# A decoder on one core: the FFN's first weight tile rounded in the GLA stage, router weights as left operand, the first scatter of zeros left out, and some reorderings in the attention stage

## The reference, cut to what matters

```python
def rms_norm(x, g):
    xf = x.astype(jnp.float32)
    y = xf * lax.rsqrt(jnp.mean(xf * xf, axis=-1, keepdims=True) + RMS_EPS)
    return (y * g.astype(jnp.float32)).astype(x.dtype)

def swiglu(h, w_gate, w_up, w_down):
    return (jax.nn.silu(h @ w_gate) * (h @ w_up)) @ w_down

def moe_swiglu(h, w_router, w_gate, w_up, w_down):
    logits = (h @ w_router).astype(jnp.float32)
    top_val, top_idx = lax.top_k(logits, TOP_K)            # 2 of 8
    top_w = jax.nn.softmax(top_val, axis=-1)
    gates = jnp.sum(jax.nn.one_hot(top_idx, N_EXPERTS, dtype=jnp.float32) * top_w[..., None], axis=-2)
    out = jnp.zeros_like(h)
    for e in range(N_EXPERTS):
        y = swiglu(h, w_gate[e], w_up[e], w_down[e])
        out = out + gates[..., e:e + 1].astype(h.dtype) * y
    return out
# first block, per layer: h = h + mixer(rms_norm(h)); h = h + ffn_or_moe(rms_norm(h))
```

## Time and profile before

| | |
|---|---|
| median of 3 runs (lowest, highest) | 2160.39 us (2160.05, 2161.13) |
| the profiled execution: its time, its span | 2161.18 us, 2159.4 us |
| PE, DVE, ACT busy, share of the span | 98%, 76%, 65% |
| mean granted TensorE clock | 0.992 |

### The profile page before, as it was taken

The page is one execution under the profiler, slowest core; times in us unless marked ns, Lnnn a source line. Parts: engine busy times, 40 slices in busy tenths (PEclk is TensorE's granted clock), DMA queues, the critical chain, the costliest instruction groups (busy, mean ns, idle before and its releaser), DMA issues.

```text
span 2159.4 us, 26580 instructions
## 1 busy us (share of the span) xinstructions
PE 2114.2 (98%) x10002; PEld 1732.1 (80%) x10003; DVE 1647.9 (76%) x2373; ACT 1397.8 (65%) x2006; POOL 25.5 (1%) x28
## 2 busy tenths in 40 slices
PE   8999999989999999999999999989999999999998
PEld 6778888778888888888888888878778788787886
DVE  5655556779999999999999999985656776565675
ACT  6554447467777777777777777765446665455664
POOL 0000000000000000000000000000110000020000
PEclk9999999989999999999999999999999999999999
DMA  6345543269999899999999899954434445443433
GB/s 270 136 168 189 195 176 137 78 269 374 372 358 386 328 376 355 367 343 371 374 354 370 339 376 360 371 206 156 167 136 140 144 170 181 176 148 136 147 139 115
DMA packets 77510, 537.24 MB, mean 249 GB/s; under 512 B 10672, under 2 KB 10928, under 8 KB 12736
## 3 DMA queue, kind: packets, MB, share of 16 engines
q1 hardware_dynamic: 77088, 535.38, 66.1%
q10 hardware_dynamic: 288, 0.10, 0.0%
HBM read 534.40 MB, written 1.05 MB: 248 GB/s over the span
## 4 chain that ended last, share of the span: by engine, by line
PE 95%; DVE 3%; ACT 1%; issue 1%; DMA 0%; ACTq 0%; DVEq 0%
PE bank L235 28%; PE bank L237 28%; PE bank L236 28%; PE bank L755 4%; PE bank L2488 1%; PE bank L2487 1%; PE bank L1845 1%; PE bank L1869 1%; DVE w_low L210 1%; DVE w_low L213 0%; PE bank L2533 0%; PE bank L2532 0%; DVE xT_low L480 0%; ACT xT_high L470 0%; PE bank L2531 0%
## 5 line engine op out<-in xcount | busy, mean ns | idle before, releaser
L235 PE MATMUL bank<-w_high,xT_high 128*128 128x512 f32 x1072 | 429.9, 401 | 12.1 <-DVE w_low L210 5.8
L210 DVE TENSOR_TENSOR w_low<-ring,w_high 128x1024 fp32r<-128x1024 f32 x232 | 285.3, 1230 | 188.3 <-ACT w_high L202 183.2
L237 PE MATMUL bank<-w_high,xT_low 128*128 128x512 f32 x1072 | 421.1, 393 | 0.0
L236 PE MATMUL bank<-w_low,xT_high 128*128 128x512 f32 x1072 | 420.5, 392 | 0.0
L202 ACT ACTIVATE w_high<-ring 128x1024 fp32r<-128x1024 f32 x232 | 245.4, 1058 | 219.7 <-PE bank L237 210.1
L235 PE MATMUL bank<-w_high,moe_x_high 128*128 128x512 f32 x896 | 359.0, 401 | 1.8 <-DVE moe_x_low L1861 1.8
L237 PE MATMUL bank<-w_high,moe_x_low 128*128 128x512 f32 x896 | 350.4, 391 | 0.0
L236 PE MATMUL bank<-w_low,moe_x_high 128*128 128x512 f32 x896 | 349.7, 390 | 0.0
L213 DVE TENSOR_TENSOR w_low<-ring,w_high 128x1024 fp32r<-128x1024 f32 x232 | 284.8, 1228 | 0.0
L235 PEld LDWEIGHTS bank<-w_high,xT_high 128*128 128x128 f32 x1072 | 203.3, 190 | 57.5 <-issue 10.4
L205 ACT ACTIVATE w_high<-ring 128x1024 fp32r<-128x1024 f32 x232 | 243.0, 1047 | 0.0
(11 more groups left out here) (345 smaller groups left out, 3119.5 us busy)
## 6 DMA issues: line engine op xcount, KB each, us to landing
moe_ring<-in_moe_tiles SPq DMA_DIRECT2D x144, 1024.0 KB, 5.6
ring<-in_hy_tiles SPq DMA_DIRECT2D x103, 1024.0 KB, 4.7
ring<-in_moe_tiles SPq DMA_DIRECT2D x96, 1024.0 KB, 5.5
ring_wide<-in_moe_tiles SPq DMA_DIRECT2D x96, 1024.0 KB, 5.6
ring<-in_ffn_tiles SPq DMA_DIRECT2D x17, 1024.0 KB, 4.8
ring_wide<-in_ffn_tiles SPq DMA_DIRECT2D x16, 1024.0 KB, 4.8
ring_wide<-in_gla_in_tiles SPq DMA_DIRECT2D x6, 1024.0 KB, 8.9
ring<-in_sb_in_tiles SPq DMA_DIRECT2D x6, 1024.0 KB, 4.8
```

The lines of the kernel that those rows point to most:

```text
L210: self.nc.vector.tensor_tensor(self.low[:, place, FIRST], memory[:, FIRST], self.high[:, place, FIRST].bitcast(F32), ALU.subtract).then_in ...
L235: nc.tensor.matmul(out, x[0], w[0], start=start, stop=False, **more)
L236: nc.tensor.matmul(out, x[0], w[1], start=False, stop=False, **more)
L237: return nc.tensor.matmul(out, x[1], w[0], start=False, stop=stop, **more)
```

## The change

What it does, by place:

- **GLA's end**: ACT and DVE do tile 16 (the FFN's first) ahead of turning h's first half.
- **FFN's start**: TensorE transposes h's second half after half of `gate_up(0, 0)` (row group 0). ACT and DVE do only tile 17 ahead of the squares and of h's second half; root and reciprocal follow, and only then tile 18.
- **Attention**: DVE's `block_out(3)` comes ahead of tile 9's split, `take_k(2)` and `scaled(2)` ahead of tile 10's, `take_q(2)` ahead of tile 10's rounding. The last values go ahead of the third part of the output product on TensorE, and `o_high`, `o_low` ahead of the last tile on ACT and DVE.
- **Route**: the router's 8 columns become the stationary operand, 256 columns of xT are streamed: 24 matmuls, which give the logits transposed (8 x 256). DVE copies them out, TensorE transposes them back (2 small ones). DVE does comparisons before it makes the rows; ACT does its exponential before it rounds the rows; the rows' low parts come after the selection matrix.
- **Experts**: the first gather goes by row groups: all 16 matmuls of the first half of every bank by t=0, then t=1, and then the same for the second half. The zeroing on DVE, the scatter of zeros and its additions are gone.

```diff
@@ GLA: act
-                tiles(16)
+                tiles(17)
                 tail.act(act, 0)
@@ ffn: pe, gate_up
+                        if (c, half, t) == (0, 0, 0):
+                            head.pe(pe, 1)
...
                     gate_up(c, 0)
-                    if c == 0:
-                        head.pe(pe, 1)
-                    else:
+                    if c:
                         turn(c - 1)
@@ ffn: act (dve alike, with total, dve, dve_rest)
-                W.prepare(act, "act", first + SPLIT)
+                W.prepare(act, "act", first + 2)
                 head.squares(act, 1)
                 head.act(act, 1)
+                head.act_rest(act)
+                head.scaled(act)
+                W.prepare(act, "act", first + SPLIT)
...
-                    if c == 0:
-                        head.act_rest(act)
-                        head.scaled(act)
@@ stick_breaking: pe
-                tile_out(1, 0, 0)
                 values(2)
                 values(3)
+                tile_out(1, 0, 0)
@@ stick_breaking: act
+                take_q(2)
                 tiles(11)
-                take_q(2)
...
-                tiles(16)
                 o_high(2)
                 o_high(3)
+                tiles(16)
@@ stick_breaking: dve
                 stayed(0)
+                block_out(3)
                 tiles(10)
                 stayed(1)
-                block_out(3)
+                take_k(2)
                 weighed(0)
                 weighed(1)
+                scaled(2)
                 tiles(11)
-                take_k(2)
-                scaled(2)
...
-                tiles(16)
                 o_low(2)
                 o_low(3)
+                tiles(16)
@@ moe: gather, first pair only
+            if by_rows:
+                for odd in range(2):
+                    for t in range(TT):
+                        pe.wait_ge(K.s_xn, t + 1)
+                        for g, b in enumerate(GATHERED):
+                            for i in range(2):
+                                last = nc.tensor.matmul(B[b][:, odd * 2 * P:(odd + 1) * 2 * P], rows[i][:, t, (2 * g + odd) * P:(2 * g + odd + 1) * P],
+                                                        sel[:, t, :], start=((i, t) == (0, 0)), stop=((i, t) == (1, 1)))
+                            if odd and t:
+                                last.then_inc(G.gath, 1)
+                return
@@ moe: dve
-                for x in y:
-                    nc.vector.memset(x[:].bitcast(F32), 0.0).then_inc(G.yv, 1)
-                nc.vector.memset(selT[:].bitcast(F32), 0.0).then_inc(G.gst, 1)
@@ moe: pe (dve alike; the counts in the waits follow)
-                    pe_run(pe, G, pair, pair, lambda: scatter(pe, G, pair * 2), ...)
-                scatter(pe, G, E)
+                    pe_run(pe, G, pair, pair, lambda: scatter(pe, G, pair * 2 - 1) if pair else None, ...)
+                scatter(pe, G, E - 1)
@@ route: pe
+                for k in range(KC):
+                    if k % 4 == 0:
+                        for t in range(TT):
+                            head.operand(pe, k // 4, t)
+                    last = matmul3(nc, B[0][0:E, 0:S], tuple(w[:, k, :] for w in K.wr), tuple(x[:, k, :] for x in K.xT),
+                                   start=(k == 0), stop=(k == KC - 1))
+                last.then_inc(s_mm, 1)
+                pe.wait_ge(s_lgT, 1)
                 for t in range(TT):
-                    for k in range(KC):
...
+                    last = nc.tensor.transpose(B[1][:, 4 * E + t * E:4 * E + (t + 1) * E], lgT[:, t * P:(t + 1) * P], K.ident[0:E, 0:E])
@@ route: dve
+                dve.wait_ge(s_mm, 1)
+                nc.vector.tensor_copy(lgT[:], B[0][0:E, 0:S]).then_inc(s_lgT, 1)
                 head.scaled(dve)
...   (logits, comparisons and choice as before; then:)
+                for t in range(TT):
+                    nc.vector.scalar_tensor_tensor(out=K.xn[:, t, :], ...).then_inc(s_rows, 1)
...   (slot numbers, selection matrix; then:)
+                for t in range(TT):
+                    dve.wait_ge(s_high, t + 1)
+                    nc.vector.tensor_tensor(rows[1][:, t, :], ..., ALU.subtract).then_inc(s_xn, 1)
```

More of the change, by code:

```diff
@@ L1349, in add @@
                     nc.vector.tensor_tensor(hv, B[2 * t + n][:], hv, ALU.add).then_inc(f["added"], 1)
-                W.prepare(dve, "dve", first + SPLIT)
+                W.prepare(dve, "dve", first + 2)
                 head.total(dve)
                 head.dve(dve, 1)
+                head.dve_rest(dve)
+                head.scaled(dve)
+                W.prepare(dve, "dve", first + SPLIT)
                 for c in range(N):
@@ L1763, with __init__ @@
 class ExpertSems:
-    def __init__(self, nc, ctx, prefix, stream, first, value, start):
+    def __init__(self, nc, ctx, prefix, stream, first, value, scattered_before):
         (self.sel, self.gath, self.xh, self.xg, self.silu, self.hid, self.tp, self.hh, self.hT, self.ya, self.yv, self.gps,
@@ L1931, in turn_sel @@
             def turn_sel(q):
-                if G.start:
-                    pe.wait_ge(G.add, n * 8 + 4 * q + 4)
-                elif q:
-                    pe.wait_ge(G.add, n * 8 + 4)
+                if G.scattered_before(n, q):
+                    pe.wait_ge(G.add, n * 8 + 4 * q)
                 mine = sel[:, :, q * P:(q + 1) * P].bitcast(F32)
@@ L1950, in pe_run @@
                     pe.wait_ge(G.hT, n * STEPS + N + 1)
-                    scatter(pe, G, n * 2 + G.start)
+                    scatter(pe, G, n * 2)
                 if s == STEPS - 1:
```

57 lines of the change are left out of this document (24 added, 33 removed).

## The result

| | before | after |
|---|---|---|
| median (lowest, highest), 4 runs each | 2160.22 us (2160.05, 2161.13) | 2146.90 us (2146.68, 2147.99) |
| the profiled execution: time, span | 2161.18, 2159.4 | 2147.04, 2145.2 |
| mean granted TensorE clock | 0.992 | 0.995 |

First, the page of after, part 1, beside the earlier trace rows: PE's share is as before, with 30 matmuls fewer.

A forecast was written before the change was run, and what follows sets the result against it. TensorE, busy 98% of the span, was taken as the bound. Gains of 4.2 (FFN), 3.9 (attention), 2.0 (route) and 2.1 (zeros), less 0.1, took 2160.4 to 2148.3 us; range 2145.8 to 2152.0.

The forecast's parts named there:

- FFN's start: At the FFN's start: two PE waits and a slow stretch go, a 1.9 us wait on hid comes; gain 4.2 us.
- Table switches: Rival at the FFN's start: ACT's two table switches hold it longer, hid 2.6 us later, 2150.9 us; chance 0.04.
- Attention: In the attention's middle and end: reordering removes PE's waits; gain 3.9 us, from 2.6 to 4.1.
- score(3)'s 0.4 of margin: In the attention: take_k(3) ends at 392.5, score(3) wants it at 392.9; missed, it costs up to 1 us.
- Route: From router to first expert matmul: earlier logits and gather bring that matmul from 463.98 to 462.0; gain 2.0 us.
- slow for 3.8 us, then 0.12 each: In the first gather: the old matmul rhythm is assumed to stay, putting the 26th matmul at 459.9.
- Zeros: At the experts' start: 8 matmuls fewer give 1.8 us, and a shorter wait for hid makes it 2.1 us.
- without them it isn't the limit: In the route: the memsets (2.1 us) were in DVE's way; once gone, DVE does not limit the first expert matmul.
- The slow clock: Rival in gather and FFN: gather stays slow, 1.8 us; FFN's new wait adds 1.5; 2149.8 to 2151.6 us; chance 0.20.
- the better case: Rival: clock up early in the gather, x at 461.6, FFN's hid half a us sooner; 2147.0 us; chance 0.10.
- Experts at DMA's pace: Rival in the experts' stage: DMA sets the pace, first refill 2.4 us earlier, not 4.1; 2150.0 us; chance 0.05.
- splits that lag: Rival in the experts' stage: DVE's split work exceeds PE's step and the lag stays; 2168 us at 102%; chance 0.01.

The follow-up runs named there:

- f_tile: The changed kernel with tile 16 rounded and split in the FFN's program again, the new order there kept; 2151.23 us.
- silu_first: The changed kernel with the first silu and hidden ahead of tile 19's rounding and split in the FFN; 2146.98 us.
- the five siblings: u_att2, u_att1, f_tile, silu_first and u_ffn: the changed kernel's route, instruction for instruction, with edits elsewhere; slower gathers; medians 2146.98 to 2152.71 us.
- u_route: The changed kernel with the whole route part undone (48 narrow matmuls, old order, gather by banks), zeros still left out; 2148.13 us.
- b_nozero: The kernel before with only the zeroing, the scatter of zeros and its additions removed; 2157.78 us, ratio 0.9986.
- u_ffn: The changed kernel with its FFN part undone: tile 16 rounded in the FFN's program again, old order there; 2152.71 us.
- u_att1: The changed kernel with the attention's middle undone (block_out(3), take_k(2), scaled(2), take_q(2) in their old places); 2151.07 us.
- u_att2: The changed kernel with the attention's end undone (output product's third part ahead of the last values, last tile's split ahead of the last output split); 2149.54 us.
- u_zero: The changed kernel with the memsets, the scatter of zeros and its additions put back; 2153.90 us.
- r_prod: The changed kernel with only the router's product undone (48 matmuls, xT stationary, 8 columns streamed), new order and gather kept; 2150.56 us.

## Why the prediction was right, and where not

- **FFN's start: right, 4.35 for 4.2.** The chain was forecast stone by stone, and each came within 0.2 us of its place once the 0.8 of the start is added back: transposes 134.32 (134.3), copies 134.96 (135.0), tiles from 138.88 (139.0), load 142.8 (142.9), hid 144.61 (144.8), PE 145.15 (145.3). The new wait is 1.59 (1.9). No slow stretch followed it. f_tile shows that tile 16's early rounding removes exactly the w_low wait, and silu_first that tile 19 ahead of the silu makes the new one. The prediction names ACT's queue alone; DVE's split of that tile ends at the same moment.
- **Table switches: the rival fell.** Both loads took 1.28 us, and the next activation began 1.30 behind each load's start; the loads themselves began within 0.02 us of the end of what stood ahead of them. So there is no time for the 1.38 us of drain that the Trainium skill (ScalarE: Activation LUTs, What ACT_TABLE_LOAD costs) adds.
- **Attention: right, 4.18 for 3.9.** turn(2) came 1.63 earlier (1.7), score(2) 2.44 (2.5), and the end gave 1.74 (1.4). That last term was taken as the wait's 1.41 alone. A wait is counted from the modelled end of the matmul before it, while in a dense run the next starts 0.16 sooner (0.23 behind a start, for 0.39 of duration), and the first one behind the wait takes 0.34 to the next instead of 0.23: 0.3 in all. score(3)'s 0.4 of margin held.
- **Route: the places right, 2.64 for 2.0, but the gain is mostly not the route's.** Behind R the logits came at 5.34 (forecast 5.65), the counts at 7.28 (7.55), the gather at 12.17 (12.40), the first expert matmul at 18.89 (19.55). The trip to PE and back took 0.86 us, from 437.59 to 438.45, where 1.1 were taken. The larger half, 0.4, is the term "slow for 3.8 us, then 0.12 each": it was 3.1. That is luck and not a fact of the change; in the five siblings the same route came out at 19.49 to 20.06, which is 1.5 to 2.0 us of gain. And u_route, with the old route and no zeros, has its first expert matmul at 20.00: 1.53 of the 2.64 come without any edit to the route.
- **Zeros: the whole is 3 us, not 2.1, and the prediction split it wrongly.** It counted PE's 1.8 and the waits (the new wait of 0.3 on hidden didn't come), and put the memsets under the route, where "without them it isn't the limit". b_nozero shows that in the old order they were the limit: from the gather to the first expert matmul their going gave 2.06 of the part's 3.4 us in place (1.63 by u_route, which is the same route in another place). By cause the 5.0 read from R to hidden's transposes are 3.3 for the zeros (b_nozero, 32.26 to 29.00) and 1.8 for the route on top of it (to 27.24), against 2.1 and 2.0 forecast. As the forecast removed both, its sum of 4.1 came near all the same, and nearer still to the 3.8 to 4.4 of the five siblings.
- **Parts undone sum to more than the whole.** By the ratios u_ffn, u_att1, u_att2, u_route and u_zero cost 5.2, 3.2, 1.9, 1.3 and 6.5 us, 18 for a gain of 13.3. In their profiles each of the first three has 0.6 to 1.2 of a slower gather in it, and u_zero has 3.65 at the experts' end, 1.2 of the gather and 1.5 of the slow stretch behind it. Each is good to 2 to 4 us either way, so the sum is loose as well.
- **The slow clock (0.20)** was right that the clock can take a part back, and half right on how: never behind the FFN's new wait, often in the gather. Its price of 1.8 had 0.8 for the gather's last steps and 1.0 for the experts' first us. In u_ffn, slow to the gather's end, the first expert matmul came 0.5 behind the forecast's place (20.06 for 19.55), and the clock was up behind it; in u_zero it fell again there, and that cost 1.5. After's own execution was nearer to the better case (the rival at 0.10, 2147.0): the clock was up at 3.1 us, but hid came only 0.2 sooner.
- **A slip without effect.** The prediction speaks of six waits that the diff touches and lists eight; its sums use them all.
- **Experts at DMA's pace, and splits that lag: no.** The distance from hidden's first transposes to the end is the same within 0.2 us, at a DMA share of 0.96 as before.

## What to carry to other kernels

A chain read instruction by instruction from the old timeline, with the new order laid over it, gave nearly each new place within 0.3 us; what it can't give is the clock behind an idle stretch, about 1 us in the gather here, so leave that much room. Work that adds nothing numerically (zeros scattered for uniformity) costs not only its own pass but its place in the queue of the engine that prepares it. And before crediting one edit, put it alone into the kernel before as well as taking it alone out of the kernel after: for the zeros the medians said 3.0 and 6.5 us. A forecast sum that comes true doesn't show that its terms did: route and zeros summed well and were split wrongly.

## What the runs showed of the hardware

- **The moment at which TensorE speeds up again isn't set by the code around it alone.** Six kernels with the same route, one trace each, had it 3.1 to 6.1 us behind the same start. It moved an unchanged stretch by 1.2 us, and in the profile it took back 1.1 of the 1.87 us that silu_first won. The moment of the fall moved too: 2.6 to 5.0 us behind R in the four kernels with the old product.
- **A matmul with 8 streamed columns takes as long as one with 256**: at the full clock both start 0.11 apart (442.45 to 443.68 in before, 435.88 to 437.12 in after). So the router's product with its columns streamed, 48 matmuls instead of 24, takes twice the time, and on top of it the clock fell inside it in all four kernels that have it (36 matmuls took 7 us at 0.57 in r_prod), and in none of the ten with the other form.
- **At the span's start the pace and the recorded clock disagree.** Before's window 11 to 14.9 has matmuls 0.43 apart, yet 1.00 as its granted clock; the same pace at 1440 to 1445 in after shows 0.50. There the timeline is to be read, not the clock. (Windows of before, then of after.)

```profile
11.00:14.90 3.90, 3.90 (x10) 3.03 (x10) 2.20 (x3) 2.49 (x5) 0.00 (x0) 1.00 1.00 424
```

```profile
1440.00:1445.00 5.00, 5.00 (x13) 3.84 (x13) 0.71 (x4) 1.73 (x6) 0.00 (x0) 0.50 0.01 3
```

- **Open: 3.65 us at u_zero's experts' end.** PE starts its transposes 4.29 us behind the last thing that it could have waited for, DVE's last addition; one weight load comes at 1441.48, the next only at 1445.10. Two transfers of the instruction queues lie in that gap (between 1441.8 and 1443.0), while in after none lies between DVE's last addition (its end at 1435.34) and PE's start at 1435.90. A late load of code would fit; no run tested it.
